# Wide down products: the high weights take high and low rows in one product of 512 columns

## The reference, cut to what matters

```python
def swiglu(h, w13, w2):
    g, u = jnp.split(h @ w13, 2, axis=-1)
    return (jax.nn.silu(g) * u) @ w2
...
        x = x + y
        x = x + swiglu(rmsnorm(x, norm_ffn_g[i]), f_w13[i], f_w2[i])
```

## Time and profile before

| | |
|---|---|
| median of 3 runs | 1797.13 us (1794.29 to 1799.27) |
| span of the profiled execution | 1795.4 us |
| TensorE (PE) busy | 1740.3 us, 97% of the span, 13776 products |
| VectorE (DVE) busy | 1228.8 us, 68% |
| ScalarE (ACT) busy | 974.9 us, 54% |
| mean granted TensorE clock | 0.990 |
| HBM read | 288.03 MB, 161 GB/s over the span |

### The profile page before, as it was taken

The page is one execution under the profiler, slowest core; times in us unless marked ns, Lnnn a source line. Parts: engine busy times, 40 slices in busy tenths (PEclk is TensorE's granted clock), DMA queues, the critical chain, the costliest instruction groups (busy, mean ns, idle before and its releaser), DMA issues.

```text
span 1795.4 us, 37239 instructions
## 1 busy us (share of the span) xinstructions
PE 1740.3 (97%) x13776; PEld 1647.1 (92%) x13776; DVE 1228.8 (68%) x2013; ACT 974.9 (54%) x1352; POOL 12.8 (1%) x20
## 2 busy tenths in 40 slices
PE   7999999998999999999999999999999999999997
PEld 7999999998999988569999999999999877799997
DVE  6886666587766587888666588666566665576654
ACT  4467744365775454207774446775454644467742
POOL 0000200000000000000000000000000000000000
PEclk9999999999999999999999999999999999999999
DMA  6567564533766554105566456657454431256661
GB/s 208 166 202 223 187 223 132 160 107 97 245 192 209 165 165 140 60 1 177 186 195 204 149 169 181 199 181 241 152 176 141 137 133 60 72 175 187 187 215 66
DMA packets 79545, 290.15 MB, mean 162 GB/s; under 512 B 9739, under 2 KB 12140, under 8 KB 79340
## 3 DMA queue, kind: packets, MB, share of 16 engines
q1 hardware_dynamic: 79468, 289.11, 51.3%
HBM read 288.03 MB, written 1.05 MB: 161 GB/s over the span
## 4 chain that ended last, share of the span: by engine, by line
PE 86%; DVE 9%; ACT 2%; issue 2%; DVEq 0%; DMA 0%; SPq 0%; ACTq 0%
PE bank L521 25%; PE bank L523 24%; PE bank L522 24%; DVE wlo L1464 2%; PE bank L809 2%; PE bank L796 1%; PE bank L750 1%; DVE rinv L1470 1%; PE bank L905 1%; PE bank L1001 1%; DVE conv_cv L1572 1%; ACT whi L1098 1%; PE bank L974 1%; PE bank L1011 1%; PE bank L730 1%
## 5 line engine op out<-in xcount | busy, mean ns | idle before, releaser
L521 PE MATMUL bank<-xh,whi 128*128 128x256 f32 (+1 forms) x2736 | 776.2, 284 | 7.5 <-DVE wlo L1464 7.3
L522 PE MATMUL bank<-xl,whi 128*128 128x256 f32 (+1 forms) x2736 | 771.2, 282 | 0.0
L523 PE MATMUL bank<-xh,wlo 128*128 128x256 f32 (+1 forms) x2736 | 770.6, 282 | 0.0
L1098 ACT CAST whi<-raw 128x1024 fp32r<-128x1024 f32 (+1 forms) x490 | 538.4, 1100 | 363.5 <-PE bank L523 324.1
L1464 DVE TENSOR_TENSOR wlo<-raw,whi 128x1024 fp32r<-128x1024 f32 (+1 forms) x491 | 629.6, 1282 | 4.8 <-ACT whi L1098 2.7
L521 PEld LDWEIGHTS bank<-xh,whi 128*128 128x128 f32 x2736 | 517.5, 189 | 24.0 <-DVE wlo L1464 12.4
L523 PEld LDWEIGHTS bank<-xh,wlo 128*128 128x128 f32 x2736 | 518.3, 189 | 0.0
L522 PEld LDWEIGHTS bank<-xl,whi 128*128 128x128 f32 x2736 | 514.7, 188 | 1.3 <-issue 1.2
L521 PE MATMUL bank<-ffn_hh,whi 128*128 128x256 f32 x880 | 246.7, 280 | 0.0
L523 PE MATMUL bank<-ffn_hh,wlo 128*128 128x256 f32 x880 | 246.7, 280 | 0.0
L522 PE MATMUL bank<-ffn_hl,whi 128*128 128x256 f32 x880 | 245.8, 279 | 0.0
(11 more groups left out here) (322 smaller groups left out, 2028.5 us busy)
## 6 DMA issues: line engine op xcount, KB each, us to landing
raw<-in_w SPq DMA_DIRECT2D x414, 512.0 KB, 3.6
raw<-in_w SPq DMA_DIRECT2D x80, 704.0 KB, 4.2
att_bias<-in_bias SPq DMA_DIRECT2D x4, 512.0 KB, 5.5
hy_w<-in_filt_w SPq DMA_DIRECT2D x8, 256.0 KB, 5.2
hy_decay<-in_decay SPq DMA_DIRECT2D x4, 512.0 KB, 4.4
mla_uq<-in_uq SPq DMA_DIRECT2D x1, 1152.0 KB, 5.3
x<-in_xT SPq DMA_DIRECT2D x1, 1024.0 KB, 5.8
out<-x SPq DMA_DIRECT2D x8, 128.0 KB, 2.0
```

The lines of the kernel that those rows point to most:

```text
L521: pe.matmul(ps, whi[:, slot, wc], hi[:, k, cols], start=first, stop=False)
L522: pe.matmul(ps, whi[:, slot, wc], lo[:, k, cols], start=False, stop=False)
L523: mm = pe.matmul(ps, wlo[:, slot, wc], hi[:, k, cols], start=False, stop=last)
L1098: nc.scalar.copy(whi[:, p % RING, 0:k * P], raw[:, p % RING, 0:k * P]).then_inc(panel_hi, 1)
```

## The change

Three things change.

1. **Rows.** The rows of 256 columns get arrays of their own with a pitch of 256 float32, 1,024 bytes (`xq_h`, `xq_l`, and `yh`, `yl` in every stage), with gaps behind them so that what follows keeps its place. `xh` and `xl` at pitch 272 stay for the 272-column products and overlay `xq`. Two pads (96 and 48 float32) shift the arrays: the weight slots start at a multiple of 512 bytes (before: 128 bytes past one), every row of 256 columns at a multiple of 256 bytes.
2. **Down products.** `ffn_hh` and `ffn_hl` become one array `ffn_h` of 22 chunks by 2 by 256: high and low rows of a chunk lie side by side. The high weights take both in one product of 512 columns, which fills the bank: high by high in its first half, high by low in the second. The low weights take the high rows as before (256 columns, first half). A chunk has two products in place of three, with the same 768 columns.
3. **Adding up.** Per down tile VectorE adds the second half of the bank to `x` first, waits for that through its own semaphore (`link`), and then adds the first half as before.

```diff
+    sb("align_weights", [P, 96])
+    def rows(name, n):
+        return [(name, [P, n, SEQ], F32R), (name + "_gap", [P, n * META], F32)]
...
+    xq = overlay("xq", rows("h", C) + rows("l", C))
     xh = sb("xh", [P, C, L], F32R)
...
+    sb("align_rows", [P, 48])
...
-    ffn = overlay("ffn", [("hh", [P, FC, L], F32R), ("hl", [P, FC, L], F32R)])
-    Y = [("yh", [P, C, L], F32R), ("yl", [P, C, L], F32R)]
+    ffn = overlay("ffn", [("h", [P, FC, 2, SEQ], F32R), ("gap", [P, 2 * FC * META], F32)])
+    Y = rows("yh", C) + rows("yl", C)
...
+    def split_of(cols):
+        return (xq["h"], xq["l"], Q) if cols == A else (xh, xl, B)
...
                     last = k == (FC - 1 if ph.k == K11 else len(ks) - 1)
+                    if ph.k == K11:
+
+                        wide = bank[(ph.b0 + tile) % 4][:]
+                        if first:
+                            pe.matmul(wide, whi[:, slot, wc], hi[:, k, :, :], start=True, stop=False)
+                        pe.matmul(ps, wlo[:, slot, wc], hi[:, k, 0, :], start=False, stop=False)
+                        if not first:
+                            mm = pe.matmul(wide, whi[:, slot, wc], hi[:, k, :, :], start=False, stop=last)
+                        w += 1
+                        continue
...
-            product(f"down{layer}", ffn["hh"], ffn["hl"], A, (hid_lo, FC * layer))
+            product(f"down{layer}", ffn["h"], None, Q, (hid_lo, FC * layer))
...
                     dve.wait_ge(panel_used, ph.p0 + j + 1 + 4 * i)
+                    if half:
+                        link(V.tensor_tensor(x[:, m, cols], x[:, m, cols], bank[(ph.b0 + tile) % 4][:, SEQ:2 * SEQ],
+                                             ALU.add))
                     V.tensor_tensor(x[:, m, cols], x[:, m, cols], bank[(ph.b0 + tile) % 4][:, w],
                                     ALU.add).then_inc(bank_free, 1)
...
-            dve_steps(ph, 0, ph.n, step)
+            if ph.k == K11:
+                dve_steps(ph, 0, ph.n, step, link, 2)
+            else:
+                dve_steps(ph, 0, ph.n, step)
```

More of the change, by code:

```diff
@@ L561, in product @@
             if norm is not None:
-                first_panels(ph, hi, lo, cols, ready, norm, cols)
+                first_panels(ph, hi, lo, cols, ready, norm, A)
                 for j in range(2, 4):
@@ L681, in out_slices @@
                         wc = slice(k * P, (k + 1) * P)
-                        pe.matmul(ps, whi[:, slot, wc], at["yh"][:, k, A], start=k == 0, stop=False)
-                        pe.matmul(ps, whi[:, slot, wc], at["yl"][:, k, A], start=False, stop=False)
-                        mm = pe.matmul(ps, wlo[:, slot, wc], at["yh"][:, k, A], start=False, stop=k == C - 1)
+                        pe.matmul(ps, whi[:, slot, wc], at["yh"][:, k, Q], start=k == 0, stop=False)
+                        pe.matmul(ps, whi[:, slot, wc], at["yl"][:, k, Q], start=False, stop=False)
+                        mm = pe.matmul(ps, wlo[:, slot, wc], at["yh"][:, k, Q], start=False, stop=k == C - 1)
                         if k == C - 1:
                             mm.then_inc(panel_used, 1)
-            first_panels(ph, xh, xl, A, (x_lo, C * norm), norm, A)
+            first_panels(ph, xq["h"], xq["l"], Q, (x_lo, C * norm), norm, A)
             pe.wait_ge(na["loaded"], 16)
             for m in range(2, 16):
-                panel(ph, 0, m, xh, xl, A, None)
+                panel(ph, 0, m, xq["h"], xq["l"], Q, None)
                 if m >= 2:
@@ L697, in attention @@
                 if t < 8:
-                    panel(ph, 0, 16 + t, xh, xl, A, None,
+                    panel(ph, 0, 16 + t, xq["h"], xq["l"], Q, None,
                           (ATT_V[t % 2], ph.t0 + 16 + t + (1 if t < 2 else 3)))
@@ L713, in attention @@
             for j in range(2, 8):
-                panel(PH["out1"], j // 4, j % 4, at["yh"], at["yl"], A, None)
+                panel(PH["out1"], j // 4, j % 4, at["yh"], at["yl"], Q, None)
         def hyena(norm):
@@ L785, in hyena @@
             ph = PH["in2"]
-            first_panels(ph, xh, xl, A, (x_lo, C * norm), norm, A)
+            first_panels(ph, xq["h"], xq["l"], Q, (x_lo, C * norm), norm, A)
             for j in range(2, 4):
-                panel(ph, 0, j, xh, xl, A, None)
+                panel(ph, 0, j, xq["h"], xq["l"], Q, None)
             def spectra(u):
@@ L813, in hyena @@
             for p in range(4, 24):
-                panel(ph, p // 4, p % 4, xh, xl, A, None)
+                panel(ph, p // 4, p % 4, xq["h"], xq["l"], Q, None)
                 if p in (4, 13):
@@ L846, in hyena @@
             for j in range(3, 8):
-                panel(PH["out2"], j // 4, j % 4, hy["yh"], hy["yl"], A, None)
+                panel(PH["out2"], j // 4, j % 4, hy["yh"], hy["yl"], Q, None)
         def retention_in(norm):
@@ L982, in latent @@
                     ro = PH["ret_out"]
-                    panel(ro, 0, t - 2, rt["yh"], rt["yl"], A, None, (5, ro.t0 + t + 2))
+                    panel(ro, 0, t - 2, rt["yh"], rt["yl"], Q, None, (5, ro.t0 + t + 2))
                 if h < MH:
@@ L1036, in _ @@
             else:
-                product(f"in{layer}", xh, xl, A, (x_lo, C * norm), norm)
+                product(f"in{layer}", xq["h"], xq["l"], Q, (x_lo, C * norm), norm)
             if layer == 0:
@@ L1050, in _ @@
         latent()
-        product("mla_out", ml["yh"], ml["yl"], A, None)
-        product("w_o", mg["yh2"], mg["yl2"], A, (y_lo, YBASE["mrg"]))
-        product("up4", xh, xl, A, (x_lo, C * norm), norm)
+        product("mla_out", ml["yh"], ml["yl"], Q, None)
+        product("w_o", mg["yh2"], mg["yl2"], Q, (y_lo, YBASE["mrg"]))
+        product("up4", xq["h"], xq["l"], Q, (x_lo, C * norm), norm)
         norm += 1
-        product("down4", ffn["hh"], ffn["hl"], A, (hid_lo, FC * DEPTH))
+        product("down4", ffn["h"], None, Q, (hid_lo, FC * DEPTH))
         total(norm, A)
@@ L1805, in hyena @@
                     if order:
[L1806 removed]
+                        y_from_bank(hy, cc, dst, Q, YBASE["in2"])
                 if n == 0:
@@ L1924, in latent @@
                     dve.wait_ge(ms["out"], h + 1)
-                    y_from_bank(ml, h // 2, bank[2][:, Q], A, YBASE["mla"])
+                    y_from_bank(ml, h // 2, bank[2][:, Q], Q, YBASE["mla"])
                 h = t - 2
```

45 lines of the change are left out of this document (23 added, 22 removed).

## The result

| | before | after |
|---|---|---|
| median | 1795.96 us, 4 runs (1794.29 to 1799.27) | 1807.13 us, 4 runs (1806.60 to 1813.14) |
| span of the profiled execution | 1795.4 us | 1805.2 us |

The ratio after to before is 1.0072, with a 95% interval of 1.0051 to 1.0092: slower by 0.7% (the two medians alone give 1.0062). The forecast was 1791.4 us.

What follows compares the result with a forecast made beforehand. TensorE, busy 97% of the span, was taken as the bound: number of products by their pace, plus the norms between phases. Terms -4.9 + 2.3 - 3.1 = -5.7 us took 1797.1 to 1791.4 us; own range 1784 to 1798, over all 1768 to 1815.

Steps and rivals of the forecast that it cites:

- Term 3: Split products on aligned rows: 0.3 ns faster each over 10,450 products, 3.1 us saved.
- rival B: Aligned rows slow every split product, `up` and `in` phases from 118.1 to 120 ns; at 2 ns 1815.4 us; chance 0.20.
- Term 1: Wide product in the five down phases: 229.8 ns, a chunk 347.5 against 353.1, 4.9 us saved over 880 chunks.
- rival D: Down phases: a wide product costs two narrow ones, 235.4 ns, giving 1796.3 us; chance 0.10.
- 272-column row: Profile evidence: ten steps of 126.0 ns each, excess 12.7 ns, at or above an excess in proportion to columns.
- float32 rows: Profile evidence: plain float32 products of 512 and 256 columns, read as a fixed excess of 2.6 to 2.7 ns.
- Term 2: VectorE's second add per down tile: hidden except at the last tile, 5 x 0.46 = 2.3 us lost.
- The covers: Other engines' work stays hidden behind TensorE: adds, panel loads, the tile's end; no new clock pause above 0.46 us.
- The excess as a matter of fetching: Split products' time beyond their columns, 11.0 to 11.4 ns: rows or weights fetched too slowly for 2.4 GHz.
- A: Rival: aligned rows quicken every split product, by 2 ns, 20.9 us saved, giving 1773.6 us; chance 0.23.

## Why the prediction was wrong

| rows of 256 | three narrow products | wide product, second add |
|---|---|---|
| pitch 1,088 bytes (before) | 1 | 1.0001 (0.9991 to 1.0010) |
| at the weights' place (the change) | 1.0094 (1.0080 to 1.0109) | 1.0072 (1.0051 to 1.0092) |
| 192 bytes past it | 0.9799 (0.9774 to 0.9824) | 0.9849 (0.9832 to 0.9866) |

Read down a column for the places, along a line for the wide product.

- **Term 3, the addresses, is the step that failed, in sign and in size.** It took -0.3 ns a product; measured was +1.67 wherever split products outside the down phases follow each other without idle time. The ground that failed is that a row in four pieces of 256 bytes is fetched quicker than one in five. Rows that all lie in four pieces (distance 0) take 120.0 ns, and rows at 192, which lie in five, take 113.3: the distance to the weights decides, and equal places are among the slowest. The mechanism was on record as rival B, "what was a slow step for one start of four is now every step", with 120 ns in the `up` phases, and that is what came. Its reason against, "fewer pieces to fetch", should not have carried weight, since no row showed it. B's time of 1815.4 was too high: 9,570 x 1.67 = 16 us are on offer, but of the some 15 us that the stretches would have grown 2.3 belong to the norms, as part of the stages wait for other engines; 4.5 us were given back by the clock, which is luck; and the low-weight products did not slow down (116.7 ns).
- **Term 1, the wide product, was mis-sized.** Forecast were 229.8 + 117.7 = 347.5 ns a chunk, 5.6 less than before. Measured was 236.7 + 116.7 = 353.3 in the change; counted alike over a phase, a chunk is 0.9 ns quicker than before there and 2.9 on the rows of before. This is rival D: the excess goes with the columns. The 272-column row had said so. Halving the excess was a compromise between that row and the float32 rows. These were no guide: they take 215.8 ns for 256 columns, nearly twice as long, and at half the rate the split products have no excess either. Of the forecast 4.9 us the change's own down phases gave about 0.7, and 2.4 on the old rows.
- **Term 2, the second add, was about right:** 0.46 us between the adds at the two places shown. Each of the five norms ends 0.5 to 0.65 us later, 0.12 of it for the wide last product, whose end the prediction took to be no later than counted. On the old rows -2.4 + 2.3 = -0.1 us fits the measured ratio, whose interval is -1.6 to +1.8 us.
- **The covers held.** VectorE is 37.80 us busy in a 62.30 us window of `down0`, the clock there is full, and DMA has 0% of the chain:

```profile
239.60:301.90 62.30, 62.30 (x359) 54.31 (x359) 37.80 (x50) 26.75 (x33) 0.00 (x0) 1.00 0.55 180
```

- **The excess as a matter of fetching** The earlier trace rows fits the runs, which move it by addresses alone, and A's sign was possible too: there was more to win than A's 2 ns, at another place. The prediction saw the stake (10 us for 1 ns) and called the term its likeliest mistake, and yet took a side on it.
- The Trainium skill, SBUF — State Buffer, "Who interferes with whom", gives TensorE two independent read ports, one for the rows and one for the weights, and says that it never waits on anyone. As to the other engines the runs agree: with them idle the pace is the same. Independent of each other the two streams are not here: with TensorE alone at work the pace goes from 113.3 to 120.0 ns by the place of rows against weights. The rule of the Trainium skill, TensorE: Matmul & The Clock Gate, "Wait — 56ns, not 53.3ns?" (N / 2.4 + about 2.5 ns), fits the plain float32 products if each column counts twice (512 / 2.4 + 2.5 = 215.8 ns, and 215.8 was measured). It gives 109.2 ns for the split ones, which took 113.3 or more at every place tried.

## What to carry to other kernels

When products follow each other without idle time, and each loads its own weights, take the pace from start to start and compare it with columns / 2.4 GHz; if it lies above, move rows against weights by a pad before merging or reordering anything, and time several distances at the width that you use: for 256 columns alignment to the same boundary was the slowest of the usual ones here, for 512 it was the best of four. Where one layout has two rhythms, time it often. A change that alters layout and instructions together should be priced, and tried, as two changes: here the layout cost 0.9%, the wide product nothing on the old layout, and rows 192 bytes past the weights' place with narrow products gave 2.0% over before.

## What the runs showed that was not expected

- A stream of split rows paid at the least 1/16 over its columns: 113.33 ns for 256, 226.67 for 512. With 128 and 192 columns and their own 128x128 weights the products took 111.67 ns alike, at the one place tried.
- The distance from weights to rows, in a grid of 256 bytes, is worth up to 5.9% of a product of 256 columns: 113.33 ns at 112 and 192 bytes, 120.00 at 0. Rows 4 bytes past the grid cost 123.33. For 512 columns the order is another: 226.67 at 0, 233.33 at 192.
- At a distance of 192 bytes there are two steady rhythms, 113.33 and 117.8 ns, for the same instructions at the same addresses. A phase keeps its rhythm until TensorE pauses. Other places showed two paces as well (116.67 and 118.62 ns at 16).
- PSUM banks in turn, and a sum of its own for each product, changed nothing at the places of the changed kernel (120.00 ns both).
- Some ten microseconds more or less at TensorE's lower clock (an estimate from the granted clocks of the three pieces above) are worth 4.5 us between two executions, nearly half of the difference between these two kernels' spans.
